# First modulation computed in two halves of the features, and normalized rows stored for the expert gather, in a two-layer hybrid diffusion kernel

## The reference

```
mod = silu(cond) @ ada_w[l] + ada_b[l]          # (1024) x (1024, 6144): 25 MB of weights for a layer
u   = h * (1 + m[1]) + m[0]                     # modulated input of the mixer
y   = attn_gla_mixer(u, ...)                    # layer 0: one projection u @ w_in (1024 x 2336), window attention, GLA, output projection
y   = short_conv_mixer(u, ...)                  # layer 1
h   = layer_norm(alpha * h + m[2] * y) * ln_w + ln_b
tokens = h * (1 + m[4]) + m[3]
y   = hier_moe(tokens)                          # best of 4 groups, best 2 of its 8 experts; 32 experts, 201 MB of weights for a layer
h   = layer_norm(alpha * h + m[5] * y) * ln_w + ln_b
```

## Time and profile before

| | us |
|---|---|
| time, median of 3 runs (lowest to highest) | 2299.51 (2298.70 to 2300.08) |
| profiled execution: time | 2300.38 |
| profiled execution: span, first to last instruction | 2298.5 |
| PE busy in the span | 2174.1 (95%) |
| DVE busy | 807.6 (35%) |
| ACT busy | 405.3 (18%) |
| POOL busy | 360.6 (16%) |

### The profile page before, as it was taken

One profiled execution on the slowest core, in us unless ns is written; L12 is line 12 of the kernel. 1 busy time (PEld: TensorE's weight loads), 2 busy tenths in 40 slices (PEclk: granted clock), 3 DMA queues, 4 the chain that ended last, 5 costly groups with the idle time before them and its releaser, 6 DMA issues.

```text
span 2298.5 us, 27962 instructions
## 1 busy us (share of the span) xinstructions
PE 2174.1 (95%) x10576; PEld 1049.9 (46%) x10576; DVE 807.6 (35%) x1709; ACT 405.3 (18%) x864; POOL 360.6 (16%) x386
## 2 busy tenths in 40 slices
PE   6999998999998999999997999999998999999996
PEld 3546545777554343334432444444553343334432
DVE  2694214556626311111111633434455111111114
ACT  2301142554211111010111410100111100110112
POOL 0000012222122100101000423221321010201003
PEclk8999999999999999999999999999999999999998
DMA  9892000001425999999998411114326999999997
GB/s 388 329 370 80 1 0 1 2 2 38 149 92 208 394 419 419 420 411 419 411 420 352 172 37 55 37 55 163 142 110 266 416 419 419 405 419 419 414 395 297
DMA packets 135816, 572.50 MB, mean 249 GB/s; under 512 B 25049, under 2 KB 38521, under 8 KB 93690
## 3 DMA queue, kind: packets, MB, share of 16 engines
q1 hardware_dynamic: 123002, 537.04, 58.9%
q0 software_dynamic: 12672, 33.57, 3.7%
HBM read 548.52 MB, written 34.62 MB: 254 GB/s over the span
## 4 chain that ended last, share of the span: by engine, by line
PE 79%; DMA 7%; DVE 6%; SPq 4%; issue 3%; ACT 1%; DVEq 0%; POOLq 0%; ACTq 0%
PE bank L1284 21%; PE bank L1360 12%; PE bank L1308 10%; PE bank L864 10%; PE bank L1199 5%; PE bank L1156 5%; DMA bigA<-in_moe_w 4%; SPq L543 3%; PE bank L815 3%; DVE lnwb L1777 2%; PE bank L950 1%; PE bank L967 1%; PE bank L1420 1%; PE bank L1141 1%; PE bank L981 1%
## 5 line engine op out<-in xcount | busy, mean ns | idle before, releaser
L1284 PE MATMUL bank<-bigA,bigB 128*32 128x512 f32 (+2 forms) x1888 | 479.7, 600 | 15.4 <-DMA bigA<-in_moe_w 10.6
L864 PE MATMUL bank<-bigC,bigB 128*128 128x512 f32 (+3 forms) x768 | 292.8, 537 | 0.0
L1284 PEld LDWEIGHTS bank<-bigA,bigB 128*32 128x32 f32 (+2 forms) x1888 | 157.8, 133 | 237.6 <-issue 230.0
L1308 PE MATMUL bank<-bigA,bigB 128*32 128x512 f32 (+2 forms) x912 | 242.5, 594 | 3.6 <-DVE bigB L2222 3.1
L864 PEld LDWEIGHTS bank<-bigC,bigB 128*128 128x128 f32 x768 | 142.4, 192 | 128.0 <-issue 119.8
L1284 PE MATMUL bank<-bigC,bigB 128*32 128x512 f32 (+2 forms) x560 | 171.4, 593 | 0.0
L1360 PE MATMUL bank<-bigB,bigA 128*128 128x512 f32 x384 | 170.7, 592 | 0.0
L1474 ACT ACTIVATE bigB<-bank,small 128x128 f32<-128x128 f32 x280 | 104.6, 460 | 369.8 <-PE bank L815 369.7
L2542 POOL DMA_INDIRECT y_rows<-bigB,ints x42 | 42.4, 1010 | 810.5 <-DVE bigB L2227 790.3
L2218 DVE TENSOR_TENSOR bigB<-bigB,bank 128x512 f32<-128x512 f32 x42 | 28.9, 688 | 306.4 <-PE bank L1284 306.4
L2227 DVE TENSOR_TENSOR bigB<-bank,gate 128x512 f32<-128x512 f32 x84 | 54.1, 686 | 234.3 <-PE bank L1308 234.3
(11 more groups left out here) (347 smaller groups left out, 2623.6 us busy)
## 6 DMA issues: line engine op xcount, KB each, us to landing
bigA<-in_moe_w SPq DMA_DIRECT2D x250, 1024.0 KB, 24.6
bigC<-in_moe_w SPq DMA_DIRECT2D x80, 1024.0 KB, 23.3
bigA<-in_ada_w SPq DMA_DIRECT2D x40, 1024.0 KB, 6.8
misc<-in_moe_w SPq DMA_DIRECT2D x36, 1024.0 KB, 24.1
lnwb<-in_moe_w SPq DMA_DIRECT2D x18, 1024.0 KB
bigA<-y_rows SPq DMA_DIRECT2D x14, 1024.0 KB, 11.9
bigA<-in_w_in_odd SPq DMA_DIRECT2D x12, 1024.0 KB, 5.4
bigA<-in_ada_w SPq DMA_DIRECT2D x4, 2048.0 KB, 13.8
```

The costliest lines, as they stand in the source:

```text
L864: last = mm(bank(n % 3)[:, 0:w], uT[:, k, t * P:(t + 1) * P], wring[:, g % 2, k, at_:at_ + w], start=(k == 0), stop=(k == KC - 1))
L1284: last = mm(bank(m)[at_:at_ + w, :], xT[:, j, KC // 2 * h + k, at_:at_ + w], w13_at(SLOT_OF[m, h, q][0], k), start=(h == 0 and k == 0), st ...
L1308: last = mm(bank(6 + n)[at_:at_ + w, :], gT[:, 2 * h + k, at_:at_ + w], w2_at(SLOT_OF[2, h, q][0], k)[:, n * 512:(n + 1) * 512], start=(h ...
```

## The change

**The start.** `ada_first` comes in eight parts of 1 MB (half of the k blocks by 512 columns, in runs of 2 KB): four parts of the first 512 features (h = 0: shift and scale, two halves of the k blocks) and four of the second (h = 1). The rows of a half are made with two column groups of PE for each part, the bias enters by a matmul (`first_bias`), and the columns of each half are made by themselves. Units 0 to 2 (`HALVED`) run in halves: features of h = 0 first. `w_in` of group 0 comes in two halves as well. The first two parts of h = 1 and the last two share two semaphores (`ada_half0`, `ada_half1`), two transfers on each.

PE's start before, by line: 829 rows, 836 columns, 815 transposes, 864 units, 876 partial sums.

The diff, cut to its core:

```diff
-        sums_after = {8 + 3 * (i // 2) + i % 2: i for i in range(20)}
+        HALVED = 3
+        sums_after = {7 + 3 * (i // 2) + i % 2 + (i >= 16): i for i in range(20)}
...
             def x_tile(t):
                 if t >= 3:
-                    sp.wait_ge(S("u_T"), t - 2)
+                    sp.wait_ge(S("u_T"), t + 1)
...
+            def first_part(h, n):
+
+                k, m = 4 * (n // 2), n % 2
+                load(ada_first[:, h, n], ada_k[0][:, k:k + 4, D * m + 512 * h:D * m + 512 * h + 512],
+                     f"ada_half{n % 2}" if h else f"ada_in{n}")
...
+            w_in(0, 0, KC // 2)
+            x_tile(1)
+            x_tile(2)
+            for n in range(4):
+                first_part(1, n)
+            w_in(0, KC // 2, KC)
...
             def ada_part(n):
 
-                if n == 0:
-                    sp.wait_ge(S("ada_mm"), 1)
+                if n < 2:
+                    sp.wait_ge(S("ada_mm"), 1 + 2 * n)
...
+            def store_normed(l, t):
+                sp.wait_ge(S("nrm"), 2 * l * NT + t + 1)
+                sp.dma_start(z_dram[l][t * P:(t + 1) * P, :], hh[:, t]).then_inc(S("normed_out"), 16)
...
-                sp.wait_ge(S("nrm"), (2 * l + 1) * NT)
-                for n in ((5, 6), (8, 9))[l]:
-                    piece(l, n)
-                store(l, NT - 1)
-                for n in ((7, 8, 9, 18), (18,))[l]:
+                if l:
+                    store(l, NT - 2)
+                store_normed(l, NT - 1)
+                for n in ((5, 6, 7, 8, 9), (8, 9))[l]:
                     piece(l, n)
...
                 sp.wait_ge(S(f"xg_in{l}_0"), 16)
                 sp.wait_ge(S("route_mm"), 9 * l + 3)
+                store(l, NT - 1)
                 piece(l, 11)
                 piece_in_rows(l, 15)
+                piece(l, 18)
...
+            def first_rows(h, q0, q1):
...
+                for q in range(q0, q1):
+                    m = q % 2
+                    pe.wait_ge(S(f"ada_half{q % 2}" if h else f"ada_in{q}"), 32 if h else 16)
+                    for k in range(4 * (q // 2), 4 * (q // 2) + 4):
+                        n = 2 * (k % 2) + m
+                        last = mm(bank(3)[32 * n:32 * n + 32, :], cond[:, k, :], ada_first[:, h, q, k % 4, :],
+                                  start=(k == 1), stop=(k >= KC - 2), skip_group_check=True)
...
+            first_rows(0, 0, 4)
+            x_T_half(0, 0)
+            first_columns(0)
+            unit_half(0, 0)
+            first_rows(1, 0, 2)
+            x_T_half(1, 0)
+            unit_half(1, 0)
+            first_rows(1, 2, 4)
+            x_T_half(2, 0)
+            x_T_half(0, 1)
+            x_T_half(1, 1)
+            first_columns(1)
+            unit_half(2, 0)
+            x_T_half(2, 1)
+            unit_half(0, 1)
+            unit_half(1, 1)
+            x_T(HALVED)
+            unit_half(2, 1)
...
                 ln_stats(0, t)
+                if t == NT - 1:
+                    router_rows(0, t)
                 ln_scale(0, t)
             count(4, SEL)
-            router_rows(0, NT - 1)
             moe(0)
...
-                pool.wait_ge(S("nrm"), 2 * NT * l + t + 1)
+                pool.wait_ge(S("normed_out"), 16 * (NT * l + t + 1))
...
                 gather(0, first_tok)
+                ln(l, NT - 1)
                 pool.wait_ge(S("routed"), 8 * l + 7)
```

More of the change, by code:

```diff
@@ L696, in _ @@
                 piece(0, n)
-            for t in (4, 5):
-                store(0, t)
+            store(0, 5)
+            store_normed(0, NT - 2)
             piece_in_rows(0, 14)
@@ L824, in _ @@
             pe.wait_ge(S("cond_ok"), 1)
-            for k in range(KC):
-                if k % 2 == 0:
-                    pe.wait_ge(S(f"ada_in{k // 2}"), 16)
-                for n in range(4):
-                    last = mm(bank(0)[32 * n:32 * n + 32, :], cond[:, k, :], ada_first[:, k, n * 512:(n + 1) * 512],
-                              start=(k == 0), stop=(k == KC - 1))
-            last.then_inc(S("ada_mm"), 1)
-            pe.wait_ge(S("const_in"), 16)
-            pe.wait_ge(S("cond_a"), 2)
@@ new lines, in _ @@
+            pe.wait_ge(S("cond_in"), 48)
+            def first_rows(h, q0, q1):
+                if h and q0 == 0:
+                    pe.wait_ge(S("cond_a"), 2)
+                for m in range(2 if q0 == 0 else 0):
+                    mm(bank(3)[32 * m:32 * m + 32, :], cc("ones")[0:1, 0:32], first_bias[:, m * D + 512 * h:m * D + 512 * h + 512],
+                       start=True, stop=False, skip_group_check=True)
+                for q in range(q0, q1):
[5 more added lines that the diff above has]
+                                  start=(k == 1), stop=(k >= KC - 2), skip_group_check=True)
+                if q1 == 4:
+                    last.then_inc(S("ada_mm"), 1)
@@ new lines, in first_columns, with u_ready @@
+            def first_columns(h):
+                pe.wait_ge(S("cond_a"), 2 + h)
+                for k in range(4):
+                    last = mm(bank(7)[:, 16 * h + 4 * k:16 * h + 4 * k + 4], mrow[:, h, k * P:(k + 1) * P], cc("pick")[:, 0:4],
+                              start=True, stop=True, skip_group_check=True)
+                last.then_inc(S("ada_mm"), 1)
+            def u_ready(t, h=1):
+                if t >= HALVED:
+                    pe.wait_ge(S("u_ev"), 2 * t - 2)
+                elif t == 1:
+                    pe.wait_ge(S("u_ev"), h + 1)
+                else:
+                    pe.wait_ge(S("u_ev_d"), 2 * h + t // 2 + 1)
@@ L919, in decay_gates @@
                         .then_inc(S("gate_mm"), 1)
-            x_T(0)
-            x_T(1)
-            for n in range(len(units)):
-                unit(n)
+            first_rows(0, 0, 4)
[16 more added lines that the diff above has]
+            unit_half(2, 1)
+            for n in range(HALVED - 1, len(units)):
+                if n >= HALVED:
+                    unit(n)
                 if n + 2 < NTC:
@@ L1595, in _ @@
             act.wait_ge(S("ms_ok"), NT // 2)
-            go(rms, ms, ACT.Sqrt, bias=epsc[:, 1:2], scale=1.0 / DV).then_inc(S("rms_a"), 1)
+            go(rms, ms, ACT.Sqrt, bias=epsc[:, 1:2], scale=1.0 / DV).then_inc(S("root"), 1)
             def ln(norm, t, src):
@@ L2584, in moe @@
                 run_over(pool, n_over, block_of)
-            for t in range(NT):
+            for t in range(NT - 1):
                 ln(0, t)
```

172 lines of the change are left out of this document (97 added, 75 removed).

## The result

The changed kernel took 2303.84 us in the median (2301.46 to 2305.93, 20 runs), the kernel before 2299.54 in the runs beside it: a ratio of 1.0018, with a 95% interval of 1.0012 to 1.0024, or 4.3 us more: a small loss, but not nothing. The forecast was 2302.0.

What follows compares the result with a forecast made beforehand. Bounds: PE's units and the partial sums behind them, DVE ending last, in the first 175 us; DMA in the expert stage. 2300.38 + 2.8 - 0.5 = 2302.7, at the median 2301.8, stated as 2302.0; range 2296.5 to 2308.

Steps and rivals of the forecast that it cites:

- The start: First stage: DVE's last wait that matters ends 6.2 - 3.4 = 2.8 us late, a term of +2.8.
- the turn: Turn to the experts: -0.5 us in layer 0 and 0 in layer 1.
- the hole: Start, DMA queue: dry at 38.5, data again at 45.7, a hole of 7 us where before there was none.
- `ada_mm` = 3: Start: the count SP waits for ahead of `ada_part(1)`, forecast at 43.0 us.
- DVE's wait at 110.16: Start: DVE's last wait that matters, forecast to end 2.8 us late, DVE then running without waiting.
- PE's 5.1 us of waits for DVE: End of the first stage: PE's two waits for DVE, forecast to absorb PE's own 6.2 us of lateness.
- the row of `w_in`: Start, loads: profile rate of 388 GB/s for runs of 2 KB, taken for the new parts.
- The rival of the clock: Start: PE's clock falls to half from 31 us, +3 to +6.8 on the hole, total 2305 to 2309; chance 0.30.
- the 1.5 that the sum allows for handoffs: Start: estimate of 1.5 us for handoffs between DMA, PE and ACT, taking 41.5 to 43.0.
- The rival that nothing would happen at the start: Start: earlier partial sums cover the lateness whole, stage 0, total 2299.0; chance 0.13.
- DVE lost 3.6 behind it: Turn, layer 0: POOL's affine pair behind the gather holds up DVE's table instructions, 3.1 us lost.
- the gather's gain: Turn: the gather of step 0 starts up to 3.5 us earlier in each layer, from 1.5 and 2.0.

Runs made afterwards that it cites:

- the start alone: Kernel before with only the start changed (first modulation and units 0 to 2 in halves, new table of partial sums): 2302.66 us against 2299.42, ratio 1.0015.
- the turn alone: Kernel before with only the turn to the experts changed, the start as before: 2300.64 us against 2299.42, ratio 1.0003.
- the modulation moved out of its shadow: Changed kernel with DVE's modulation of the gathered rows moved ahead of the three table instructions before it: 2299.88 us, ratio 0.9999 to the kernel before.
- `w_in` ahead: Changed kernel with `w_in` of group 1 issued between the first and second part of `ada_w`: 2299.90 us, ratio 1.0009 to the kernel before.
- four semaphores: Changed kernel with a semaphore of its own for each of the second half's four parts: 2299.73 us, ratio 0.9999 to the kernel before.
- more fill: Changed kernel with three more filling matmuls on PE between the gathered rows' transposes and the first expert product: 2302.88 us, ratio 1.0017 to the kernel before.
- the modulation ahead in the kernel before: Kernel before with DVE's modulation of the gathered rows moved ahead of the table instructions, nothing else: 2299.55 us against 2299.36, ratio 1.0000.

## Why the prediction was right, and what was off

**The size.** The sum of the forecast was +2.3 us at the median, rounded up to 2302.0, and "the same"; measured were +4.3, within the bound of 4.6 and inside the range. Of the 2.0 that are missing, 1.7 are the turn, which was forecast with the wrong sign; that the number lies inside the range all the same says nothing for that step.

**The start, +2.8 forecast, +3.0 by the marks and +3.2 by the run of the start alone.** Nearly every step held: the hole (38.5 to 46 us), `ada_mm` = 3 (43.0 forecast, rows done at 43.70), x tile 3 (59.9, 60.64), unit 3 (67.0, 67.96), DVE's wait at 110.16 ending 2.8 late (3.06), PE's 5.1 us of waits for DVE taking up the rest (2.0 are left). The parts moved at 386 GB/s, as the row of `w_in` had it. The Trainium skill has it otherwise: by its page "DMA: Bandwidth & Descriptors", section Specifications, transfers of 512 B or more run at line rate. The trace does not agree: runs of 2 KB moved at 386 GB/s, runs of 4 KB at 418; by that rule the stage would have ended 2 us earlier, by the prediction's estimate. The run with `w_in` in the hole shows that the hole, and not PE's own gaps, was the cause.

The rival of the clock came true in part and cost little: the clock did fall twice, at 24 and at 31 us, the first time beside waits for loads that set the end anyway; the half unit behind the second took 3.70, full clock. But the row products behind the last part of h = 1 lay on the path. They ran from 33.50 to 35.88 (clock 0.80 from 33.5 to 36), 2.4 us where the sum had 0.96. That 43.0 came out so near is partly luck: the 1.5 that the sum allows for handoffs went mostly here, where the clock was below full, and not into handoffs. The rival that nothing would happen at the start fell with the 386.

**The turn, -0.5 forecast, +1.2 by the run of the turn alone.** The steps up to the product were right. The gather came 3.9 us earlier behind T7 in layer 0 (3.5 forecast), DVE lost 3.6 behind it (3.1 forecast), and the product began 1.3 earlier in layer 0 and at the same distance in layer 1. One reading behind the gather's gain was wrong: in layer 1 of the kernel before POOL did stand in DVE's way, only at another instruction:

```profile
1731.28 2.34 POOL L2528 TENSOR_TENSOR bigC<-bigC,lnwb 128x1024 f32<-128x1024 f32 x1
1731.52 2.13 DVE L2062 TENSOR_TENSOR bigB<-bigB 128x8 f32<-128x8 f32 x1
```

So about 2 us were to be had there as well, and the same gain for each layer (3.5 in layer 1 too) came out right without this having been seen. The step that failed is the one that stopped there: "DVE's path to the modulation of the gathered rows (line 1735) gains 3.5 - 3.1 = 0.4" was taken as what the stream gains. In layer 0 the transposes of the gathered rows came 5 us earlier for a product that began 1.3 earlier, in layer 1 1.2 us earlier for one that began no earlier, so PE stood 4.38 and 2.12 us. The clock was at 0.57 in the 4 us behind the first, the products took 8.78 and 8.73 instead of 7.09, and the late pieces went out 0.4 and 1.7 us later. The price of the clock had been counted for the start only. In layer 1 it was another instruction than the two named that was held up most: line 2224, 3.09 us for 32 by 32 elements, which ended with POOL's first affine instruction.

That the pair of POOL instructions is the cause is shown twice: without it, and with the modulation moved out of its shadow, the late pieces come 5.2 and 4.4 us sooner behind T7 in layer 0. In layer 1 it is 5.2 and 3.0. In the time 4.7 and 4.0 us show, most of it from layer 1, which took 570.2 and 571.7 us from T7 to the end of the span, and 574.4 in the changed kernel.

**Profile and median.** The profiled execution of the changed kernel is 2.4 us behind that of before, the medians 4.3. The profiles show one place where the two executions differ the other way. Layer 0's experts end with the sum of the scattered rows; the stretches there are, in the kernel before

```profile
1264.00:1270.00 6.00, 5.38 (x10) 1.62 (x11) 1.51 (x3) 0.54 (x2) 0.00 (x0) 0.50 1.04 415
```

and in the changed one

```profile
1264.00:1268.00 4.00, 1.70 (x4) 0.40 (x3) 0.00 (x0) 2.24 (x3) 0.00 (x0) 1.00 0.67 197
1268.00:1274.00 6.00, 5.54 (x20) 1.69 (x20) 1.82 (x5) 2.38 (x3) 0.00 (x0) 1.00 1.03 411
```

PE waited 3.51 us for the rows in the first and 2.60 in the second; behind this wait the clock was at 0.50 in the first and at 1.00 in the second. From T7 to T7 layer 0 took 995.7 us before and 993.95 in the changed kernel. With the turn alone and with `w_in` ahead the layer took 993.5 and 993.3; with four semaphores and with more fill the eight products there took 3.68 us, as in the kernel before, and the layer 996.0 and 995.6. All three kernels with the turn of before (also the start alone and the modulation ahead in the kernel before) lie at 995.5 to 995.7, nine of the eleven with the new turn at 993.1 to 994.0. So this gain of nearly 2 us can come or stay away from kernel to kernel; whether it does so from run to run, which would bring the 2.4 to 4.3, no trace here can say, since each kernel left one.

## What to carry to other kernels

When a wait is moved in a queue that issues loads in order, ask what the transfers do while it lasts: a wait that is short on PE can drain the DMA engines, and filling the hole with a load that is ready anyway costs one moved line. When data is made to arrive earlier, follow it to the engine that takes it up and look at what stands ahead there; a gain that ends in front of a busy engine becomes a wait on the next, and the wait can cost the clock. And where two engines' instructions meet, order the consumer's next needed instruction ahead of those that can be held up.

## What was not expected of the hardware

A wait of PE of 4.38 us was followed by a stretch at a granted clock of 0.57 (761 to 765 us), one of 2.6 us in the same kernel (before 1268 us) by a stretch at 1.00, and one of 2.12 in layer 1 by a product that took 8.73 us instead of 7.09; with four semaphores one of 1.31 there was followed by 7.09. The length of the last wait alone does not tell which it will be.

A DVE instruction on 32 by 32 elements (line 2224, layer 1) took 3.09 us and ended with POOL's first affine instruction, whose row begins 0.69 after its own; with the pair left out it took 0.24 at the same place beside the gather. So an instruction whose row begins first can still be held for the other's whole length; what POOL does in those 0.69 us no row shows. The rows with four semaphores and without the pair, both of layer 1:

```profile
1753.97 7.09 PE L1362 MATMUL bank<-bigA,bigB 128*64 128x512 f32 x32 [1.31 <-DVE bigB L1817]
...
1742.61 0.24 DVE L2224 SCALAR_TENSOR_TENSOR bigB<-misc,bigB 32x32 f32<-32x32 f32 x1
```
